# Two-block transformer step: where the joint copies, the pass copies and one softmax sum stand in the queues of the second attention

## The reference, cut to what matters

```
for block of queries, for head, for kind in (selected, window):
    s = q . k * scale                        # scores, keys up to the query's block
    p = softmax(where(causal, s, -inf))      # along the keys
    o += gate[kind] * (p @ v)
p_c = masked_softmax(q . k_cmp * scale)      # 31 compressed keys
o  += gate[0] * (p_c @ v_cmp)
```

## Time and profile before

| what | us |
|---|---|
| median of 3 runs | 1437.89 (1436.22 to 1438.48) |
| profiled execution | 1435.15 |
| its span, first to last instruction | 1433.3 |
| PE busy, share of the span | 1407.3, 98% |
| second attention, from the first turn to the 16th large turn | 828.83 to 960.18 |

### The profile page before, as it was taken

How to read it: one execution, slowest core, us unless ns; L and a number is a source line. 1 busy time by engine, 2 the same in 40 slices (tenths; PEclk the granted TensorE clock), 3 DMA queues, 4 the chain that set the end, 5 groups by cost and what they waited for, 6 DMA issues and landing times.

```text
span 1433.3 us, 20948 instructions
## 1 busy us (share of the span) xinstructions
PE 1407.3 (98%) x7707; PEld 1185.6 (83%) x7707; DVE 869.9 (61%) x1644; ACT 666.3 (46%) x1163; POOL 611.8 (43%) x435
## 2 busy tenths in 40 slices
PE   9999999999999999999999999899999999999998
PEld 7888889878778888899997778787888888888886
DVE  4335996566672363933466677752264878777776
ACT  5454555568573333343334567763225433323342
POOL 5433644444453444254443355653416332333330
PEclk9999999999999999999999999999999999999999
DMA  6322433203102675768672200004265433333221
GB/s 208 98 74 88 147 96 94 61 18 97 37 1 77 217 261 189 279 201 300 225 243 74 62 28 1 2 2 161 89 234 178 145 103 104 105 106 110 88 88 59
DMA packets 89114, 170.30 MB, mean 119 GB/s; under 512 B 7031, under 2 KB 22978, under 8 KB 89026
## 3 DMA queue, kind: packets, MB, share of 16 engines
q1 hardware_dynamic: 79298, 140.72, 30.9%
q10 hardware_dynamic: 9728, 28.39, 5.4%
HBM read 148.12 MB, written 20.97 MB: 118 GB/s over the span
## 4 chain that ended last, share of the span: by engine, by line
PE 90%; DVE 4%; issue 3%; ACT 1%; POOL 1%; DMA 1%; SPq 0%; POOLq 0%; DVEq 0%; ACTq 0%
PE bank L1073 57%; PE bank L1771 9%; PE bank L1359 4%; PE bank L1135 4%; PE bank L1351 4%; PE bank L1165 3%; PE bank L996 3%; PE bank L1033 1%; PE bank L1167 1%; ACT sc L2112 1%; PE bank L1759 1%; POOL w_lo L832 1%; PE bank L1590 0%; DVE xt_lo L3036 0%; DMA raw<-in_w_in 0%
## 5 line engine op out<-in xcount | busy, mean ns | idle before, releaser
L832 POOL TENSOR_TENSOR w_lo<-raw,w_hi 128x1024 fp32r<-128x1024 f32 (+3 forms) x185 | 435.0, 2360 | 488.2 <-ACT w_hi L1847 488.2
L1847 ACT ACTIVATE w_hi<-raw 128x1024 fp32r<-128x1024 f32 (+3 forms) x189 | 191.4, 1015 | 371.9 <-DMA raw<-in_w_in 171.9
L1073 PE MATMUL bank<-xt_hi,w_hi 128*128 128x512 f32 x560 | 221.5, 395 | 1.6 <-POOL w_lo L832 1.5
L1073 PE MATMUL bank<-xt_hi,w_lo 128*128 128x512 f32 x560 | 218.2, 390 | 0.0
L1073 PE MATMUL bank<-xt_lo,w_hi 128*128 128x512 f32 x560 | 218.1, 389 | 0.0
L1073 PE MATMUL bank<-w_hi,xt_hi 128*128 128x512 f32 (+2 forms) x520 | 191.3, 368 | 0.0
L1073 PE MATMUL bank<-w_lo,xt_hi 128*128 128x512 f32 (+2 forms) x520 | 189.2, 364 | 0.0
L1073 PE MATMUL bank<-w_hi,xt_lo 128*128 128x512 f32 (+2 forms) x520 | 189.2, 364 | 0.0
L1073 PEld LDWEIGHTS bank<-xt_hi,w_hi 128*128 128x128 f32 x560 | 105.2, 188 | 25.8 <-issue 4.3
L1073 PEld LDWEIGHTS bank<-xt_hi,w_lo 128*128 128x128 f32 x560 | 105.1, 188 | 22.2
L1073 PEld LDWEIGHTS bank<-xt_lo,w_hi 128*128 128x128 f32 x560 | 105.2, 188 | 21.2 <-issue 0.5
(11 more groups left out here) (457 smaller groups left out, 2939.2 us busy)
## 6 DMA issues: line engine op xcount, KB each, us to landing
raw<-in_w_in SPq DMA_DIRECT2D x72, 512.0 KB, 3.5
raw<-in_w_ff SPq DMA_DIRECT2D x36, 512.0 KB, 3.7
quarter_b<-in_w_ff SPq DMA_DIRECT2D x28, 512.0 KB, 3.5
raw<-in_w_in SPq DMA_DIRECT2D x24, 392.0 KB, 4.4
w_hi<-sums_hi SPq DMA_DIRECT2D x16, 512.0 KB, 5.3
w_lo<-sums_lo SPq DMA_DIRECT2D x16, 512.0 KB, 6.2
raw<-in_w_branch SPq DMA_DIRECT2D x12, 512.0 KB, 3.8
chunk_a<-in_w_out ACTq DMA_DIRECT2D x12, 512.0 KB, 5.2
```

The lines of the kernel that those rows point to most:

```text
L832: pool.tensor_tensor(w_lo[:, slot, 0:halves, 0:width], raw[:, slot, 0:halves, 0:width], w_hi[:, slot, 0:halves, 0:width].bitcast(F32), ALU ...
L1073: ins = pe.matmul(o, lhs, rhs, start=st and j == 0, stop=en and j == 2)
L1847: act.activation(w_hi[:, slot, 0:halves, 0:width], raw[:, slot, 0:halves, 0:width], ACT.Copy)\
```

## The change

The joint copy goes from the start of `pos % 4 == 2` to `pos % 4 == 1`: on ACT it stands before the small step's exponentials, on DVE after the small step's masks and before the reciprocals of the large and the small step. `empty` goes from position 9 after the pass's last step to the end of position 8 after it, where PE does V products. The last two entrance tiles go from the start of positions 4 and 5 to the end of positions 5 and 6. The first compressed sum goes from position 3 to position 2. PE's and POOL's lists stay as they are, and no instruction is added or removed.

```diff
-CMP_SUM, CMP_NORM, CMP_T = (3, 11, 35, 43), (5, 13, 37, 45), (11, 19, 43, 51)
+CMP_SUM, CMP_NORM, CMP_T = (2, 11, 35, 43), (5, 13, 37, 45), (11, 19, 43, 51)
... (ACT)
+                    if nsa and pos % 4 == 1:
+                        copy_turned(entry(stage, pos + 1 - lag))
-                    if pos % 2 == 0:
+                    if pos % 2 == 0 and not (nsa and pos % 4 == 2):
                         copy_turned(p)
... (DVE)
-                lag_empty = 9 if nsa else lag + 3
+                lag_empty = 8 if nsa else lag + 3
...
-                    copy_turned(entry(stage, pos - lag))
+                    if not (nsa and pos % 4 == 2):
+                        copy_turned(entry(stage, pos - lag))
                     emptied_pair = entry(stage, pos - lag_empty)
-                    if is_step(emptied_pair) and UNITS[2 * emptied_pair + 1]["last"]:
+                    pass_done = is_step(emptied_pair) and UNITS[2 * emptied_pair + 1]["last"]
+                    if pass_done and not nsa:
                         empty(UNITS[2 * emptied_pair + 1]["pas"])
                     if pos == AHEAD - 1:
                         empty_entrance(stage, (2, 3))
-                    if stage != "b" and pos in (AHEAD + 1, AHEAD + 2):
+                    if stage == "a" and pos in (AHEAD + 1, AHEAD + 2):
                         empty_entrance(stage, (pos - AHEAD - 1,))
                     if e in KEY_TURNS:
                         keep_keys(e, score_banks(stage, pos)[1])
                     if is_step(e):
                         mask_step(stage, pos)
+                    if nsa and pos % 4 == 1:
+                        copy_turned(entry(stage, pos + 1 - lag))
                     if pos != AHEAD:
                         sums_inverse(entry(stage, pos - 1))
...
+                    if nsa and pos in (AHEAD + 2, AHEAD + 3):
+                        empty_entrance(stage, (pos - AHEAD - 2,))
+                    if nsa and pass_done:
+                        empty(UNITS[2 * emptied_pair + 1]["pas"])
```

## The result

The changed kernel takes 1424.66 us, median of 6 executions (1423.35 to 1427.17). The kernel before, run beside it, now has a median of 1436.23 over 6 (1434.94 to 1438.48; the three shown above are among them). The ratio is 0.9918, 95% interval 0.9905 to 0.9930: 11.6 us less (10.1 to 13.6 by the interval), where 11.2 was forecast.

What follows compares the result with a forecast made beforehand. PE bounds the kernel, its open time mostly waits before 256 turns, released by ACT's joint copy. Cycle gains total 11.7 us, less 0.5 for later releases: 1437.89 - 11.2 = 1426.7 us, range 1425.0 to 1431.5.

Steps and rivals of the forecast that it cites:

- What bounds the kernel: In the stage PE waits before the 256 turn for ACT's joint copy, though the profile names DVE; 13.4 us to win.
- the joint copy on ACT: In a plain cycle, the wait before the 256 turn falls from 0.82 to about 0.07 us, a gain of 0.75.
- Joint copy on DVE: In a plain cycle it fills a gap 3.38 to 4.07 us after the large turn, ending before ACT's copy.
- Passes: Where the pass copy stands between DVE's large copy and masks, moving it gains 0.3 us per such cycle.
- Cycles behind compressed work: At 896.75 and 905.20, 256 turns 4.93 and 4.78 us after the large turn: gains 1.28 and 0.77, together 2.05.
- First cycle: Its 256 turn can start at 833.4 instead of 836.04; some given back, with next cycle's 0.4 a gain of 2.7 us.
- Sum: Gains of all cycles in the stage total 11.7 us; 0.5 taken off for later releases leaves 11.2.
- How the numbers follow: Chances for the whole kernel: forecast 0.78, faster in all 0.94, same 0.03, slower 0.03; range's low end 12.9 us won, high 1431.5.
- POOL as the last: DVE's joint copy stretches POOL's work; 256 turn slips 0.37 to 0.45 us in some 11 cycles: 1431.4; chance 0.07.
- Pass copies that cost what they save: Late pass copies on DVE delay large copy, small turn and masks, up to 0.6 us in 5 cycles: 1429.7; chance 0.09.
- That nothing moves: The 256 turn is held by something the view does not show, not ACT's copy: 1437.9; chance 0.03.
- The ring: POOL later than T+3.5 (T the large turn) closes a loop of in-order queues: 1.3 us a cycle, 1444; chance 0.03.

## Why the prediction was right, and where it was wrong

*What bounds the kernel, and the joint copy on ACT: right.* The central claim, that ACT's copy holds PE although the profile names DVE, is shown: DVE's copy alone gives 0.0, ACT's alone 7.0. Four plain cycles gained 0.76 to 0.78 each; 0.75 was forecast.

*Joint copy on DVE: right, and its price is now known*, 2.4 us: without it DVE's copy ends 0.3 behind ACT's in each plain cycle.

*Passes: the size right, the place not always.* Alone they gave 0.29 in each of four cycles, as forecast. With the joint copies in front only two cycles owe anything to them: 0.30 in the plain cycle that has a pass copy, as forecast, and 0.24 in one that has none, where the delay arrives from the cycle before through ACT and the compressed sum. The prediction did not see this second way.

*Cycles behind compressed work: the term that was too large.* The first came out at T+4.92 (forecast 4.93), the second at T+5.11 instead of T+4.78: 1.73 of 2.05. In the kernel before, DVE's large copy of the second of these cycles starts at T+1.35 and ACT's large exponentials at T+2.67:

```profile
901.00 0.68 DVE L2842 COPY prob_t<-bank 128x512 f32<-128x512 f32 x1
...
902.32 0.72 ACT L2112 ACTIVATE sc<-sc,negmax 128x512 f32<-128x512 f32 x1 [0.95 <-DVE negmax L2819]
```

From T+2.67 the forecast's 1.43, the joint copy and 0.10 give its T+4.78. In the changed kernel both come 0.33 later, the copy at T+1.68 (896.40, T = 894.72) and the exponentials at T+3.01, and the same steps behind them give T+5.11. The cycle before had become shorter (7.82, it was 9.11), and ACT's compressed exponential at 892.40, ahead of the 384 exponentials, now makes DVE's reciprocal wait (0.26 at 894.51), with maximum, sum and large copy behind it. With shift, exponential and sum moved, both turns come at T+4.43, so the compressed work is the cause; which of the three pieces holds how much is read from the rows, as no run moves one alone.

*First cycle: too small.* The 256 turn came at T+4.57 as forecast, but DVE's copy of the 256 step ended at T+6.96, not T+7.2, so the cycle took 7.02 instead of 7.32; with the second cycle's 0.41 the gain is 3.05, not 2.7. It is nearly independent of the rest (1.94 and 2.06). The first sum and the entrance tiles were never moved one without the other, so their shares are open.

*Sum.* 11.7 was worked out for the stage and 11.95 measured. The 0.5 taken off for later releases was not there: PE followed ACT's copy by 0.10 in the plain cycles and in the two behind compressed work, as before. That 11.7 comes so near has luck in it: 0.32 too much for the cycles behind compressed work and 0.35 too little for the first two cycles cancel.

*The step that failed is the starting time in "How the numbers follow" and in the forecast of the median.* Forecast and range both start from 1437.89, the median of three executions, as if it were exact. The text had two numbers in hand that spoke against this: the three spread over 2.3 us, and the profiled execution was 2.74 below their median. Beside the changed kernel the kernel before took 1436.23 over six, 1.66 less. The forecast of 1426.7 is 2.04 above the measured 1424.66: 1.66 of it is the start and 0.37 the gain. So the time fell below the low end, 1437.89 less 12.9, although no more than 11.6 us was won. The ratio measured, applied to 1437.89, gives 1426.1, inside the range; the forecast from the profiled execution, 1423.9, is 0.8 from its counterpart's 1424.67. Had the low end taken in the lowest start that was known, 1435.15, it would have been 1422.3. Why the first three executions came out high is not shown. The mechanism, the sign and the size of the gain stand.

*The rivals.* POOL as the last: refuted by the plain cycle, where the 256 pair takes 1.10 beside the joint copy, and it was 1.09. The Trainium skill (SBUF — State Buffer, section SBUF: two separate sides) says that only a DVE operation with two SBUF inputs or in a 2-port mode locks the port pair that it shares with GpSimd. The trace agrees again: POOL's 384 pair takes 1.74 in the changed kernel beside the shift at 887.09, and 1.30 in the version in which the shift was moved away and the same taking of scores and pass copy stand beside it. Pass copies that cost what they save: refuted, the stage is 0.56 longer without them. That nothing moves: refuted by every run with ACT's copy moved. The ring: with POOL 1.2 us later, and with ACT standing for 24.9 us, the cycles with no other work in them did not grow. POOL was done by T+2.3 and never made later than the T+3.5 that the prediction names, so the point at which the ring decides stays untested.

## What to carry to other kernels

When an engine waits for two copies on two engines, work out from the rows which one ends last and test each alone; the name in the brackets is only one of the semaphores, and what one of two moves is worth can depend on the other (here DVE's copy 0.0 alone and 2.4 behind ACT's). In a rhythm bound by one engine, an earlier place in another engine's in-order queue is free as long as what stands behind the new wait is wanted later than it comes: list that for each special cycle too, not the plain one alone. Hang a range on the spread of the baseline as well as on the mechanism.

## What the runs showed of the hardware

PE starts 0.10 us after an ACT copy that releases it and 0.06 us after a DVE copy, in the plain cycles above. GpSimd's extra multiplication of 384 columns by constants took 0.51 to 0.52 us, against 0.67 for the same size with two operands that lie in SBUF one per partition.
